# Split fp32r products for the recurrent layer's input, and one fp32r gather of 320 columns for each group of experts

## The reference, cut to what matters

```
# recurrent layer (gated delta rule), x is 256 x 1024
proj = x @ w_in                      # q, k, v: 3072 columns, z: 1024, and 16 small ones
qkv = silu(causal_depthwise_conv(q k v, conv_w))      # 4 taps along the tokens
q, k = l2_normalize(q), l2_normalize(k)
...                                  # delta rule, then o * silu(z) @ w_out

# experts, xf is 256 x 1024 after an RMS norm
top_v, top_i = top_k(xf @ w_router + b_router, 4)
xs = xf[tok]                         # the tokens of each expert, gathered
h = ragged_dot(xs, w_up, sizes) + b_up
y = ragged_dot(swiglu(h), w_down, sizes) + b_down     # summed back with the top-4 softmax weights
```

## Time and profile before

| what | us |
| --- | --- |
| median of 3 runs | 2080.33 |
| profiled execution, its own time | 2080.17 |
| its span, first to last instruction | 2078.3 |
| TensorE busy | 1972.1 |
| VectorE busy | 696.5 |
| ACT busy | 428.5 |
| recurrent input, unit 0's two halves begin | 252.88, 261.84 |
| unit 1 begins; z's first unit begins; delta rule's scores begin | 272.74; 345.99; 394.47 |
| first gather begins; first expert product | 996.54; 1006.91 |
| a group of experts, second to sixth | 126.8 |
| last expert product ends; end | 2028; 2078.3 |

### The profile page before, as it was taken

One profiled execution on the slowest core, in us unless ns is written; L12 is line 12 of the kernel. 1 busy time (PEld: TensorE's weight loads), 2 busy tenths in 40 slices (PEclk: granted clock), 3 DMA queues, 4 the chain that ended last, 5 costly groups with the idle time before them and its releaser, 6 DMA issues.

```text
span 2078.3 us, 23894 instructions
## 1 busy us (share of the span) xinstructions
PE 1972.1 (95%) x9490; PEld 1218.0 (59%) x9490; DVE 696.5 (34%) x973; ACT 428.5 (21%) x652; POOL 13.8 (1%) x21
## 2 busy tenths in 40 slices
PE   6999999999999989787899999999999999999997
PEld 4799887796599878664543444434444343444333
DVE  3655532674365531342212212132222212122122
ACT  0444332112254420252100101000110110011003
POOL 0000000000000000000000000000000000000000
PEclk9999999999999999667899999999999999999999
DMA  9444612103354552104489999899998999999990
GB/s 387 168 198 161 262 42 100 63 1 157 113 227 162 201 194 81 41 1 185 181 343 422 411 373 422 363 423 408 374 421 362 423 408 374 408 375 421 384 400 21
DMA packets 67812, 543.41 MB, mean 261 GB/s; under 512 B 7552, under 2 KB 7552, under 8 KB 10528
## 3 DMA queue, kind: packets, MB, share of 16 engines
q1 hardware_dynamic: 65296, 533.53, 63.0%
q0 software_dynamic: 2160, 7.87, 1.1%
q10 hardware_dynamic: 288, 1.05, 0.1%
HBM read 541.37 MB, written 1.05 MB: 261 GB/s over the span
## 4 chain that ended last, share of the span: by engine, by line
PE 91%; DVE 4%; ACT 2%; DMA 1%; issue 1%; POOL 0%; DVEq 0%; ACTq 0%; POOLq 0%
PE ps L1982 16%; PE ps L1968 11%; PE ps L1997 8%; PE ps L503 6%; PE ps L2011 5%; PE ps L907 3%; PE ps L1119 3%; PE ps L684 3%; PE ps L615 3%; PE ps L614 3%; PE ps L686 3%; PE ps L685 3%; PE ps L613 3%; PE ps L2073 2%; PE ps L1330 2%; PE ps L2060 1%
## 5 line engine op out<-in xcount | busy, mean ns | idle before, releaser
L1982 PE MATMUL ps<-ring,arena 128*64 128x512 f32 x1536 | 334.9, 594 | 0.0
L1982 PEld LDWEIGHTS ps<-ring,arena 128*64 128x64 f32 x1536 | 108.2, 137 | 214.3 <-issue 214.3
L2207 DVE TENSOR_SCALAR arena<-ps 128x512 f32<-128x512 f32 x40 | 27.7, 692 | 598.7 <-PE ps L1982 344.6
L1968 PE MATMUL ps<-ring,arena 128*128 128x512 f32 x512 | 223.8, 595 | 0.0
L739 DVE TENSOR_TENSOR ring_split<-ring,ring_split 128x1024 fp32r<-128x1024 f32 x128 | 154.3, 1223 | 118.3 <-ACT ring_split L788 118.3
L1997 PE MATMUL ps<-ring,arena 128*64 128x512 f32 x768 | 170.1, 595 | 0.0
L1968 PEld LDWEIGHTS ps<-ring,arena 128*128 128x128 f32 x512 | 97.9, 191 | 117.1 <-issue 115.7
L788 ACT CAST ring_split<-ring 128x1024 fp32r<-128x1024 f32 x128 | 131.5, 1046 | 139.9 <-PE ps L686 89.3
L2340 ACT ACTIVATE arena<-arena 128x512 f32<-128x512 f32 x40 | 25.2, 631 | 593.2 <-DVE arena L2207 593.2
L684 PE MATMUL ps<-arena_split,ring_split 128*128 128x256 f32 x512 | 143.8, 281 | 0.2 <-DVE ring_split L739 0.2
L685 PE MATMUL ps<-arena_split,ring_split 128*128 128x256 f32 x512 | 142.9, 279 | 0.0
(11 more groups left out here) (370 smaller groups left out, 2326.0 us busy)
## 6 DMA issues: line engine op xcount, KB each, us to landing
ring<-experts_dram SPq DMA_DIRECT2D x384, 1024.0 KB, 10.8
ring<-weights_dram SPq DMA_DIRECT2D x57, 2048.0 KB, 9.5
row_buf<-rows_dram POOLq DMA_DIRECT2D x15, 512.0 KB, 9.2
ring<-weights_dram SPq DMA_DIRECT2D x3, 1024.0 KB, 11.1
tab<-tables_dram SPq DMA_DIRECT2D x1, 2285.0 KB, 17.4
x<-tokens_dram SPq DMA_DIRECT2D x1, 1024.0 KB, 5.0
arena<-rows_dram SPq DMA_DIRECT2D x2, 512.0 KB, 18.9
xT<-weights_dram SPq DMA_DIRECT2D x1, 1024.0 KB, 6.8
```

Of the source, the lines that this page charges most:

```text
L1968: ins = T.matmul(bank(2 * half_ + m), xs_big[:, 2 * c + d, :], w[:, d, m * STEP:(m + 1) * STEP], start=False, stop=c == 3 and d == 1, skip ...
L1982: ins = T.matmul(bank(first_bank + m)[at:at + SMALL], xs_small[:, 2 * c + d, SMALL * (j - 1):SMALL * j], w[half_][:, d, m * STEP:(m + 1) * ...
```

## The change

**Recurrent layer.** Units 1 to 7 use split products like the MLPs. The counters are renamed (`part_high`, `part_low`, `part_used`) and run on from MLP to MLP over these 28 chunks, in the same four buffers. The input is split too, into `gdn_x_high` (ACT, per token tile) and `gdn_x_low` (VectorE). The units use ring slots 0 to 3 in turn. ACT makes unit n + 2's high parts around tap and SiLU of unit n, VectorE its low parts behind the convolution of unit n.

**Gather.** The big and small gathers of a group become one, of 128 + 192 = 320 columns, at the end of the third small expert of the group before. It is made of fp32r products: `pre` is split into `pre_high` (ACT, in the row buffers of the last two rows) and `pre_low` (POOL, in place), and the one-hot matrices are exact. The first group keeps two gathers at their old places, in the new form. The old one-hot matrices stay, for the sums.

**Rows.** The last two rows, whose buffers `pre_high` takes, are loaded by SP behind the experts.

Some semaphores on VectorE and one for the down bias are merged with others. The diff, cut:

```diff
 def sp_after_mlp(sp, layer, names):            # both MLPs: mlp_* -> part_*
+    at = CHUNKS_BEFORE[layer]                  # (0, MLP_CHUNKS + 28)
...
+    if len(names) > 4:
         fill(sp, names[4], 4, "part_used", at + MLP_CHUNKS)
         fill(sp, names[5], 5)
...
+def v_part_low(v, chunk, raw, buffer):
+    v.wait_ge(sem("part_high"), chunk + 1)
+    high, low = split_buffer(MLP_SPLIT_SLOT, buffer)
+    V.tensor_tensor(low, raw, high, ALU.subtract).then_inc(sem("part_low"), 1)
...
+def a_part_high(a, chunk, raw, buffer):
+    if not isinstance(chunk, int) or chunk >= MLP_BUFFERS:
+        a.wait_ge(sem("part_used"), chunk - MLP_BUFFERS + 1)
+    A.copy(split_buffer(MLP_SPLIT_SLOT, buffer)[0], raw).then_inc(sem("part_high"), 1)
...
 def pe_gdn_in(pe):                             # units 1 to 5
-    for b in range(4):
-        for k in range(KT):
-            m = T.matmul(ps[:, n % 4, b * SEQ:(b + 1) * SEQ], w[:, k * STEP + b * P:k * STEP + (b + 1) * P],
-                         xT[:, k, :], start=(k == 0), stop=(k == KT - 1))
-    m.then_inc(sem("gdn_in_psum"), 1)
+    for c in range(4):
+        high, low = parts(n, c)                # waits part_low
+        for k in range(2):
+            xs_ = gdn_x_high[:, 2 * c + k, :], gdn_x_low[:, 2 * c + k, :]
+            for b in range(4):
+                at = k * STEP + b * P
...
+                T.matmul(out_, high[:, at:at + P], xs_[0], ...)
+                T.matmul(out_, high[:, at:at + P], xs_[1], ...)
+                m = T.matmul(out_, low[:, at:at + P], xs_[0], ...)
+        m.then_inc(sem("part_used"), 1)
...
+    for c in range(4):                         # z, first half: 12 products of 512 columns a chunk
+        z(0, c)
...                                             # second half: z(1, 0), z(1, 1) | head rows | z(1, 2) | z(1, 3)
 def a_gdn_in(a):
+    def highs(n, chunks):
+        a.wait_ge(unit_full[n % 4], 16 * gdn_full[n])
+        for c in chunks:
+            a_part_high(a, gdn_chunk(n, c), gdn_raw(n, c), c)
...                                             # gdn_x_high per token tile, then
+    highs(1, range(4))
...
     for n in range(6):
         taps(n)
+        highs(n + 2, range(3))
...                                             # n == 2: exp of the decay; silu(n); squares
+        highs(n + 2, (3,))
 def v_gdn_in(v):
...                                             # gdn_x_low per token tile
+    lows(1)
...                                             # convolution n, for n == 1 the decay rows' copies
+        lows(n + 2)
...
+def gathered_block(to, c, cols):
+    at = slice(c * P, (c + 1) * P)
+    for part in (pre_high, pre_low):
+        for t in range(TILES):
+            ins = T.matmul(to, part[t][:, at], gather_hot[t][:, cols], start=part is pre_high and t == 0,
+                           stop=part is pre_low and t == 1)
+    return ins
...
+def gather(g):
+    pe.wait_ge(sem("moe_hot"), cnt(2, g, 2))
+    for c in range(KT):
+        if c >= 2:
+            pe.wait_ge(sem("moe_xs"), later(g, c - 1))
+        gathered_block(bank(2 + c % 2)[:, 0:GROUP], c, slice(0, GROUP)).then_inc(sem("moe_gathered"), 1)
...
 def up_big(g, half_, r, first=False):
     for c in range(4):
+        if half_ == 0 and not first:
+            pe.wait_ge(sem("moe_xs"), later(g, 2 * c + 2))
...
 def big(g, first=False):
     turn(g, 0, 0)
-    summed(k - 2, 3)
-    gather_small(g)
+    if first: first_gather_small()
+    else: summed(k - 2, 3)
     up_big(g, 1, 4 if first else 8)
...
 def small1(g, first=False):
     turn_onehot(onehot_small[:, 0])
-    if not last: gather_big(g + 1)
 def small3(g, last=False):
     turn_onehot(onehot_small[:, 2])
+    if not last: gather(g + 1)
...                                             # ACT, small3
+def keep(g):
+    for c in range(KT):
+        a.wait_ge(sem("moe_gathered"), later(g, c + 1))
+        A.copy(xs[:, c, :], bank(2 + c % 2)[:, 0:GROUP]).then_inc(sem("moe_xs"), 1)
...                                             # VectorE, small2: hot_big, hot_small
+        hot_big(rank_s[:, :, bass.ds(STEPS_OF * (g + 1), 1)])    # 2 comparisons of 128 x 128
+        hot_small(g + 1)                                         # 2 comparisons of 128 x 192
...
 def a_router(a):
+    A.copy(pre_high[t], pre[:, t, :]).then_inc(sem("moe_pre_high"), 1)
 # gpsimd
+    pool.wait_ge(*flag("router_psum"))
+    for t in range(TILES):
+        pool.wait_ge(sem("moe_pre_high"), t + 1)
+        G.tensor_tensor(pre_low[t], pre[:, t, :], pre_high[t], ALU.subtract).then_inc(sem("moe_pre_low"), 1)
 # sync
-    for n in range(6, 8):
-        fill(sp, f"gdn_in{n}", n - 2, "gdn_in_psum", n - 1)
-    fill(sp, "gdn_out0", 4, "gdn_z_psum", 1)
-    fill(sp, "gdn_out1", 5, "gdn_z_psum", 2)
+    fill(sp, "gdn_in4", 0, "gdn_in_psum", 1)
+    for n in range(5, GDN_UNITS):
+        fill(sp, f"gdn_in{n}", n % 4, "part_low", gdn_chunk(n - 3, 0))
+    fill(sp, "gdn_out0", 4, "part_used", gdn_chunk(GDN_UNITS, 0))
+    fill(sp, "gdn_out1", 5)
...                                             # behind the experts
+    for name in LATE:
+        sp.dma_start(row_buf[:, at % 3, :], rows[at:at + 1, :].to_broadcast((P, D))).then_inc(sem("late_rows_loaded"), 16)
```

More of the change, by code:

```diff
@@ L870, in system, with gdn_chunk, gdn_raw, parts @@
             return flat[:, (2 * h + t) * P:(2 * h + t + 1) * P]
-        def pe_gdn_in(pe):
-            w = take(pe, GDN_IN_SLOTS[0])
+        gdn_x_high = split_scratch(6144, KT, SEQ)
+        gdn_x_low = view(side_split[:].rearrange("p a b -> p (a b)"), (KT, SEQ))
+        k_squares = view(xT[:].rearrange("p k t -> p (k t)"), (TILES, D))
+        gdn_full = {}
+        def gdn_chunk(n, c):
+            return GDN_FIRST + 4 * (n - 1) + c
+        def gdn_raw(n, c):
+            return ring[:, n % 4, c * CHUNK:(c + 1) * CHUNK]
+        def pe_gdn_in(pe):
+            def parts(n, c):
+                pe.wait_ge(sem("part_low"), gdn_chunk(n, c) + 1)
+                return split_buffer(MLP_SPLIT_SLOT, c)
+            for n in range(1, GDN_UNITS):
+                gdn_full[n] = taken[n % 4] + (2 if n == 4 else 1 + n // 4)
+            w = take(pe, 0)
             for t in range(TILES):
@@ L923, in heads_out @@
                 m.then_inc(sem(done), 1)
-            w = take(pe, GDN_IN_SLOTS[6])
-            for t in range(TILES):
-                m = z(0, t, range(KT))
-            m.then_inc(sem("gdn_z_psum"), 1)
+            for c in range(4):
+                z(0, c)
+            for n in range(1, GDN_UNITS):
+                taken[n % 4] += 1
             pe.wait_ge(sem("gdn_conv"), 5)
             head_col = table("head_col")
-            for n, src in enumerate((pre, side)):
+            for n, src in enumerate((pre, k_squares)):
                 pe.wait_ge(sem("gdn_sq"), n + 1)
@@ L1815, in a_router @@
         def a_router(a):
+            a.wait_ge(sem("row_used"), places["row"]["ln2"])
+            for t in range(TILES):
+                a.wait_ge(sem(f"norm_x{t}"), count(NORMS, "rn2"))
+                A.copy(pre_high[t], pre[:, t, :]).then_inc(sem("moe_pre_high"), 1)
             a.wait_ge(*flag("router_top"))
@@ L1846, in pe_gate2 @@
                     m.then_inc(sem("last_gate_psum"), 1)
-        xs_big, xs_small = scratch(0, KT, P), scratch(1024, KT, 3 * SMALL)
+        GROUP = P + 3 * SMALL
+        xs = scratch(0, KT, GROUP)
+        gather_hot = [side_split[:, t, 512 + 32 * t:512 + 32 * t + GROUP] for t in range(TILES)]
+        pre_high = [row_split[:, places["row"][name] % 3, :] for name in LATE]
+        pre_low = [pre_split[:, t, :] for t in range(TILES)]
         gate_c, lin_c = scratch(2560, STEP), scratch(3072, STEP)
@@ L2079, in big @@
-                if not first:
+                if first:
+                    pe.wait_ge(sem("moe_xs_big"), 2 * n + 2)
+                else:
                     pe.wait_ge(sem("moe_read"), cnt(5, g, 0))
-                up_big(g, 0, 0)
+                up_big(g, 0, 0, first)
                 if not first:
@@ L2147, in small3 @@
                 turn_onehot(onehot_small[:, 2])
+                if not last:
+                    gather(g + 1)
             if n > 0:
                 pe.wait_ge(sem("moe_added"), sums_before(n, 0))
-            gather_big(0)
+            else:
+                pe.wait_ge(sem("moe_pre_low"), TILES)
+            first_gather_big()
             if n == 0:
@@ L2274, in small1, with small2 @@
                 pick_small(g, 2)
-            def small2(g):
+            def small2(g, first=False, last=False):
                 k = STEPS_OF * g + 2
@@ L2282, in small2 @@
                 pick_small(g, 3)
+                if not last:
+                    if first:
+                        v.wait_ge(sem("moe_gathered_small"), 4 * n + 4)
+                    else:
+                        v.wait_ge(sem("moe_gathered"), later(g, KT))
+                    hot_big(rank_s[:, :, bass.ds(STEPS_OF * (g + 1), 1)])
+                    hot_small(g + 1)
             def small3(g):
```

(4 more changed lines are left out.)

239 lines of the change are left out of this document (138 added, 101 removed).

## The result

The changed kernel takes 2056.68 us (median of 4 runs, 2050.68 to 2057.48), the kernel before 2080.69 beside it (2079.21 to 2085.11). The ratio is 0.9886, 95% interval 0.9859 to 0.9912: 24.0 us faster, where 36.8 were forecast. The profiled execution took 2057.48 us.

The account below looks back on a forecast made before the run. TensorE was taken to bound the kernel, at 91% of the chain, with a DMA floor under the expert groups. Savings of 16.2 + 18.2 + 2.4 = 36.8 us from 2080.2 gave 2043.4 us, range 2034 to 2055.

Parts of the forecast that it names:

- part 3: Group 0's gathers and what feeds them: 2.4 us won, 0.7 at the big gather, 1.7 at the small; bounds -4 and +5.
- Rival B: Router: GpSimd's subtractions and VectorE lock each other out, 0.9 to 3.2 us, total 2044.3 to 2046.6 us; chance 0.2.
- The gather's duration: Group 0's big gather: 32 products at 0.058 to 0.117 us, doubled at half clock, 3 to 6 us against 5.30.
- Rival E: Recurrent input: new waits drop TensorE's clock to 1.2 GHz, 11.2 us more per unit, up to 2121.8 us; chance 0.04.
- Part 1: Recurrent layer's input units 1 to 7 in split products: 16.2 us won, bounds 7 and 18.5 + 1.6.
- The wait ahead of unit 2: Recurrent input: TensorE waits about 0.6 to 2.2 us for low parts queued behind convolution 0.
- Part 2: One merged gather per expert group: 2.6 us less per transition, seven transitions, 18.2 us; group falls to 124.2 us.
- the first small gather: Group 0: 32 products of 192 columns in two banks, 3.5 us against 5.2, 1.7 won.
- Part 4: Tail: the last two rows loaded after the experts cost nothing, with 6 us of cover.
- A: Recurrent input: ACT's queue holds units to 12.6 us each, about 7 us won there, total 2052.6 us; chance 0.12.
- C: fp32r products cost a quarter of fp32 ones, 0.1085 us each, total 2035.7 us; chance 0.03.
- D: Merged gather's two banks don't overlap, 10.7 us each, 38.5 us back, total 2081.9 us, no change; chance 0.02.

Follow-up runs that it names:

- after: The changed kernel with all parts of the change, against the kernel before it: 2056.68 us, ratio 0.9886.
- before: The kernel without the change, the baseline: 2080.69 us, ratio 1.
- pool_early: Changed kernel with GpSimd's two subtractions waiting for the expert input's transposes and no longer for the router logits: 2051.74 us, ratio 0.9853.
- gdn_only: Kernel before plus only the recurrent layer's input change; gathers, expert input and GpSimd as before: 2068.90 us, ratio 0.9935.
- fp32_both: Changed kernel with group 0's two gathers in plain products again and GpSimd's subtractions behind them: 2049.99 us, ratio 0.9847.
- fp32_big: Changed kernel with only group 0's big gather in plain products, GpSimd's subtractions between its two gathers: 2050.01 us, ratio 0.9846.
- rows_early: fp32_big with the decay rows' small products ahead of unit 2, VectorE's two copies behind unit 2's low parts: 2045.25 us, ratio 0.9837.
- best: rows_early plus seven unused 512-column products in the router's waits: 2042.43 us, ratio 0.9826.
- after_again: The changed kernel once more, no edit: 2054.30 us, ratio 0.9873.
- gather_only: Kernel before plus only the new gathers, split expert input, GpSimd's subtractions and late rows; plain recurrent input units: 2068.66 us, ratio 0.9938.
- taps_first: pool_early with unit 0's ScalarE scalings and VectorE convolution ahead of the decay's small operations: 2050.50 us, ratio 0.9860.
- warm: pool_early plus seven unused 512-column products in the router's waits, four before the ranks, three before the gather: 2049.37 us, ratio 0.9853.

## Why the prediction was wrong

Its direction and its large terms held. The step that failed is part 3: "I take 0.7 us won" for the first big gather and what leads to it. It measured 5.8 us lost (6.6 in the second profile). Piece by piece, after against before: the logits 0.8 us shorter; VectorE's two held steps +3.1; the gather 7.06 against 5.30 us, +1.8; what stands between gather and first up product, still at 1.2 GHz, +1.7. This is 6.5 to 7.3 of the 10.9 to 12.2 us that the five stages fall short.

- Rival B was priced right (0.9 to 3.2 us; 3.1 measured) and given 0.2. I had the mechanism and no row for it, and left it out of the sum; pool_early shows it. That the price met is partly luck: it reckoned with one wait, and there were two, of 1.6 and 1.5 us. The Trainium skill ("SBUF — State Buffer", section "SBUF: two separate sides") describes the pair as an exclusive lock for the whole instruction; the trace agrees, for VectorE's steps end at 981.29 and 983.65 us and GpSimd's two operations at 981.27 and 983.57. My reading of who is held was too narrow: the first one held, TENSOR_SCALAR, has one SBUF input. The Trainium skill names a two-port mode of VectorE beside the two inputs in the same place; whether this operation is in it no run here shows.
- The gather's duration. The bounds of 0.058 and 0.117 us per product, doubled at the low clock, allow 7.5 us for 32, and the text cut that to "3 to 6": the upper bound left out the case of the low clock throughout. The price itself was on record in the gather before, whose 32 records are 0.213 us apart at 1.2 GHz and 0.112 at 2.4; the fp32r ones cost the same, 7.06 us in all at 1.2 GHz, so nothing could be won there. What the runs showed in place of the rest is a coupling that was in no rival: the gather's own products decide whether the clock rises. With the plain gather it rose in before, gdn_only, fp32_both, fp32_big, rows_early and best; with the fp32r one it stayed at 0.50 in after, after_again, gather_only, pool_early, taps_first and warm; with long products between them it rose. Which property of the fp32r products does this stays open. Rival E looked for a low clock in the input stage, and a little of it came there, as the next point says.
- Part 1: 14.8 and 13.6 us against 16.2, and 13.6 to 16.1 over the eight profiles whose new input has its order unchanged. Unit 3 started at 301.0 to 301.7 us, within 0.6 of the forecast. Half of these profiles have a granted clock of 0.83 between 300 and 310 us, which is rival E's sign in small: from unit 3 to unit 6 they take 35.4 to 35.5 us and not 34.0. The other four, at 1.00 there, have stages of 109.2 to 109.3 us, 15.9 to 16.1 won. The dip stands behind the 2.1 us wait ahead of unit 3 and is missing in before, gather_only, rows_early and best; that the wait brings it is a guess and not shown, for four profiles with the wait have no dip. The wait ahead of unit 2 was at most 0.5 us, for unit 1 itself ran at a lower clock (0.79 from 272 to 280 us, 0.60 in after_again) and used up the rest of it.
- Part 2: 16.4 and 17.0 us against 18.2; over the eleven profiles with the new gather the mean is 17.9 (966.9 - 949.0). Pick, gather and group came as worked out. The shortfall is a clock dip at the stage's start (0.51 from 1055.4 to 1062.3 us in the first profile); the four profiles without one there (pool_early, fp32_both, rows_early, best) take 947.8 to 948.1 us, 18.8 to 19.1 won.
- In group 0 the first small gather gained 1.4 us of 1.7. The +0.9 between up small and down big is the front of that same dip, some 55 us behind the first up product, in after, after_again and gather_only; pool_early, without it (18.0), has one earlier, inside its small gather. Why its place shifts was not settled.
- Part 4 and rivals A, C and D: tail +0.1 us, no wait ahead of units 4 to 7 (A), input products about 0.118 us apart and not 0.1085 (C), gather blocks of 0.68 us (D). As argued.

## What to carry to other kernels

A change of the kind of product in a stretch at 1.2 GHz can leave TensorE there, as it did here with 32 short fp32r products in place of 32 records of plain fp32: read the granted clock around the place first, take the price of a short product from rows of its own width at that clock, and price everything behind it at the low clock too. Elementwise work given to GpSimd was not free where VectorE's small steps stood on the path; starting it some 5 us earlier against the logits' end was worth 3 us here. And where one engine's queue orders a wait ahead of work that another needs, move the wait's producer forward (decay rows, 3.1 us) before shortening the work.

## What the runs showed of the hardware

- GpSimd's TENSOR_TENSOR of 128x1024 (two, 2.33 us each) held VectorE's TENSOR_SCALAR on 128x2 (0.17 to 1.77 us) and its TENSOR_TENSOR on 128x64 (0.23 to 1.75) in all three profiles where they met, while MAX8, MATCH_VALUE_LOAD and MATCH_REPLACE8 ran beside it at their usual 0.08 to 0.29 us.
- TensorE can show busy for 19.9 us on end at a granted clock of 0.50, when the work is fp32 products of 32 columns and fp32r ones of 128 (warm), with seven of 512 among them.
- A 128-column fp32r product costs as much as one of the two records of a plain fp32 product of that width: 0.213 us at 1.2 GHz (after, fp32_big), so the plain product is twice as dear. At 256 columns it is 3.7 times as dear (0.434 us in the kernel before against 0.117).
- A plain 32-record gather that began at a granted clock of 0.50 saw it rise 3.0 to 6.0 us later in six profiles; the fp32r gather of 32 products did not see it rise in its 6.9 us in any of six.
